# Moving the low halves of the weights by 96 bytes in SBUF: padding in a float32r decoder layer

## Chip, cores and metric

One core of one Trainium2 chip. The metric is the device time of one execution in microseconds (us), the median of several runs. Lower is better.

## What is computed

One decoder layer over 256 tokens of width 1024, in float32: a SwiGLU feed-forward (FFN) of inner width 2816, then a mixing layer with two branches (block attention and RWKV-7) fed by one projection, then a second SwiGLU, then a last RMS norm. Cut to what matters here:

```python
x = x + 0.5 * swiglu(rms_norm(x, norm_ffn1), ffn1_gate, ffn1_up, ffn1_down)
h = rms_norm(x, norm_mix)
proj = h @ w_in                      # 1024 x 5120
...
merged = sigmoid(ga) * (y_a @ proj_a) + sigmoid(gb) * (y_b @ proj_b)
x = x + merged @ w_out               # 1024 x 1024
x = x + 0.5 * swiglu(rms_norm(x, norm_ffn2), ffn2_gate, ffn2_up, ffn2_down)
out = rms_norm(x, norm_final)
```

## The kernel before

**Split products.** Activations lie transposed in SBUF, 128 features of a block on the partitions and 256 tokens along them. Every large product is made in `float32r` from split operands: a weight is `whi + wlo`, an input `hi + lo`, and three TensorE products give the sum. The helper `three` (lines 1445 to 1449) issues them:

```python
mm(dst, whi[slot][:, k_, cols], xl, start=start, stop=False)
mm(dst, wlo[slot][:, k_, cols], xh, start=False, stop=False)
return mm(dst, whi[slot][:, k_, cols], xh, start=False, stop=stop)
```

The first operand is the stationary one (128x128, loaded into the array by a weight load of its own, PEld in the profile), the second the moving one (128x256). The weight load of a product runs while the product before it streams. So the load of a `wlo` block (line 1448) runs beside the product of line 1447, whose moving operand is the low part of the input; both loads of a `whi` block run beside a product whose moving operand is the high part. Lines 1480 to 1482 and 1504 to 1506 issue the same three products through other helpers (they show as L1443), and lines 1594 to 1596 do so for the LoRA weights, which have tensors of their own. The projection chunks 10 and 11 (lines 1714 to 1716) make their result token-major: there the input block is stationary and the weight block moving.

**How many.** The program issues 4632 such products: 2112 for the gates and ups of the two FFNs, 1056 for their downs, 960 for `w_in`, 192 for `proj_a` and `proj_b`, 192 for `w_out`, 120 for LoRA. A third of them, 1544, use a low part of a weight. 1472 of these load `wlo` as the stationary operand, 40 load `lora_wlo`, and 32 have `wlo` as the moving operand.

**The feed of weights.** Weights come in chunks of up to 128x2048 elements, two slots deep. SyncE issues the load to `w_raw` (line 334), ScalarE writes `w_hi` (line 528), VectorE writes `w_lo` as `w_raw - w_hi` (line 896), TensorE multiplies. Each step waits for the one before it, and slots are freed by the `multiplied` and `lo_ready` counts.

**Where things lie.** Tensors are laid in SBUF in the order of their declaration, each rounded up to a multiple of 32 bytes per partition. What a scope frees is used again by the next scope. Every block of 128x256 elements takes 1024 bytes of a partition and every half of it 512, so a tensor's start modulo 256 is also that of all the operands in it.

| tensors | line | start | modulo 256 |
|---|---|---|---|
| `w_raw0`, `w_raw1` | 157 | 16512, 24704 | 128 |
| `w_hi0`, `w_hi1` | 158 | 32896, 41088 | 128 |
| `w_lo0`, `w_lo1` | 159 | 49280, 57472 | 128 |
| `x`, `cst` | 160, 161 | 65664, 73856 | 128 |
| `vec`; `sq`, `sqsum`, `rstd`; `bias_sb`, `idle` | 162 to 168 | from 81824 | 160; 32; 64 |
| `hhi_f`, `hlo_f` (FFN inputs) | 195, 196 | 97440, 105632 | 160 |
| `hid_hi_t`, `hid_lo_t` (inputs of the downs) | 199, 200 | 117920, 140448 | 160 |
| `hhi_m`, `hlo_m` (inputs of `w_in` and LoRA) | 229, 230 | 167072, 175264 | 160 |
| `lora_whi`, `lora_wlo` | 248, 249 | 183680, 204160 | 128 |
| `yahi`, `yalo`, `ybhi`, `yblo`, `mhi`, `mlo` | 227 to 296 | from 158880 | 160 |

So the inputs of all long products begin 32 bytes, modulo 256, behind both halves of the weights.

Of the kernel before, what the change touches and what calls it, by code (L numbers as in the profile page):

```python
# [30 lines left out]
P = 128  # L31
# [113 lines left out]
def trunk(nc, A, consts, out):  # L145
    bias_dram = nc.dram_tensor("bias_rows", (H, 16, 384), F32, kind="Internal").ap()
    with ExitStack() as ctx:
        def sb(name, shape, dt=F32, scope=ctx):
            return scope.enter_context(nc.sbuf_tensor(name, shape, dt))
# [6 lines left out]

        raw = [sb(f"w_raw{i}", [P, KD, W]) for i in range(2)]
        whi = [sb(f"w_hi{i}", [P, KD, W], F32R) for i in range(2)]
        wlo = [sb(f"w_lo{i}", [P, KD, W], F32R) for i in range(2)]
        x = sb("x", [P, KD, T])  # L160
        cst = sb("cst", [P, C_ALL])
# [3 lines left out]

        rstd = sb("rstd", [P, T + 2])
        bias_sb = sb("bias_sb", [H, 384])
        idle = sb("idle", [P, 34])

        def mat(name):  # L170
            return cst[:, CCOL[name]:CCOL[name] + P]
# [1910 lines left out]
```

## Time and profile before

| what | value |
|---|---|
| median of the runs | 635.6 us (635.54, 635.6, 636.8) |
| the profiled execution | 637.97 us, with a span of 636.1 us |
| mean granted TensorE clock in it | 0.998 |

The span runs from the first to the last instruction of the profiled execution; its own time is 1.9 us more, and 2.4 us above the median. In the rows, PE is a TensorE product, PEld a weight load, DVE VectorE, ACT ScalarE, POOL GpSimd, and L1447 is line 1447 of the kernel. The ends of products are modelled by the profiler (a product of 128x256 is shown as lasting 0.28 us, though the next starts long before that), so the pace of the products is read from their starts.

### The profile page before, as it was taken

The numbers are of one execution on the slowest core, as the hardware profiler recorded it, in microseconds if no ns is written. First come the engines' busy times: TensorE is split into PE (matmuls) and PEld (weight loads), VectorE is DVE, ScalarE is ACT, GpSimd is POOL, SyncE is SP. The second block draws the span as 40 slices with busy tenths as digits, with TensorE's granted clock in tenths as the row PEclk, the third lists the DMA queues.
The fourth block names the chain that finished last, engine by engine and source line by source line (L and its number), as shares of the span: only waits on it lengthen the run. The fifth ranks groups of instructions, "written<-read, shape, count | busy, mean of one in ns | idle before, by whom it ended". The sixth has DMA issues, their size and how long they took to land.

```text
span 636.1 us, 15459 instructions
## 1 busy us (share of the span) xinstructions
PE 625.7 (98%) x6720; PEld 611.0 (96%) x6720; DVE 421.7 (66%) x490; ACT 296.0 (47%) x343; POOL 91.3 (14%) x92
## 2 busy tenths in 40 slices
PE   9999999999999999999999999999999999999996
PEld 8899999999999999999988899999999999999996
DVE  5856887665556369968993337878766676665662
ACT  6643555443334264535556445645543344443341
POOL 0017700000114000020015423015000000000120
PEclk9999999999999999999999999999999999999999
DMA  8777566546555246684242233455655566545541
GB/s 280 235 232 209 189 198 197 182 156 203 166 185 186 85 133 199 197 180 154 69 134 70 72 100 100 133 162 172 197 178 176 178 194 198 190 161 201 170 139 66
DMA packets 100672, 105.40 MB, mean 166 GB/s; under 512 B 2244, under 2 KB 98732, under 8 KB 100628
## 3 DMA queue, kind: packets, MB, share of 16 engines
q1 hardware_dynamic: 99380, 101.47, 49.8%
q0 software_dynamic: 1088, 3.02, 2.2%
q8 instruction: 35, 0.57, 0.4%
q10 hardware_dynamic: 160, 0.27, 0.1%
q14 instruction: 9, 0.07, 0.0%
HBM read 103.50 MB, written 1.25 MB: 165 GB/s over the span
## 4 chain that ended last, share of the span: by engine, by line
PE 91%; DVE 4%; DMA 3%; ACT 1%; issue 0%; SPq 0%; DVEq 0%; ACTq 0%
PE two L1447 26%; PE two L1448 25%; PE two L1449 25%; PE two L1443 11%; DMA w_raw<-in_ffn_up 2%; DVE w_lo L896 2%; DMA x_tok<-in_x 1%; PE two L1714 1%; ACT w_hi L528 1%; PE two L1715 1%; PE two L1716 1%; DVE hlo_f L915 1%; PE two L1859 0%; DVE w_lo L906 0%; ACT KK L784 0%
## 5 line engine op out<-in xcount | busy, mean ns | idle before, releaser
L528 ACT ACTIVATE w_hi<-w_raw 128x2048 fp32r<-128x2048 f32 (+1 forms) x87 | 164.3, 1888 | 256.3 <-PE two L1449 232.0
L896 DVE TENSOR_TENSOR w_lo<-w_raw,w_hi 128x2048 fp32r<-128x2048 f32 (+1 forms) x87 | 202.5, 2328 | 86.5 <-ACT w_hi L528 86.1
L1447 PE MATMUL two<-hlo_f,w_hi 128*128 128x256 f32 x640 | 178.9, 280 | 1.6 <-DVE w_lo L896 1.6
L1449 PE MATMUL two<-hhi_f,w_hi 128*128 128x256 f32 x640 | 179.7, 281 | 0.0
L1448 PE MATMUL two<-hhi_f,w_lo 128*128 128x256 f32 x640 | 179.1, 280 | 0.0
L1447 PEld LDWEIGHTS two<-hlo_f,w_hi 128*128 128x128 f32 x640 | 120.5, 188 | 2.7 <-DVE w_lo L896 2.7
L1449 PEld LDWEIGHTS two<-hhi_f,w_hi 128*128 128x128 f32 x640 | 120.4, 188 | 0.0
L1448 PEld LDWEIGHTS two<-hhi_f,w_lo 128*128 128x128 f32 x640 | 120.3, 188 | 0.0
L1447 PE MATMUL two<-hid_lo_t,w_hi 128*128 128x256 f32 x352 | 98.9, 281 | 0.0
L1449 PE MATMUL two<-hid_hi_t,w_hi 128*128 128x256 f32 x352 | 98.6, 280 | 0.0
L1448 PE MATMUL two<-hid_hi_t,w_lo 128*128 128x256 f32 x352 | 98.4, 280 | 0.0
L1447 PE MATMUL two<-hlo_m,w_hi 128*128 128x256 f32 x288 | 83.7, 291 | 0.3 <-DVE w_lo L896 0.3
L1448 PE MATMUL two<-hhi_m,w_lo 128*128 128x256 f32 x288 | 80.6, 280 | 0.8 <-issue 0.8
L1449 PE MATMUL two<-hhi_m,w_hi 128*128 128x256 f32 x288 | 80.5, 279 | 0.0
L1447 PEld LDWEIGHTS two<-hid_lo_t,w_hi 128*128 128x128 f32 x352 | 66.2, 188 | 0.6 <-DVE w_lo L896 0.5
L1448 PEld LDWEIGHTS two<-hid_hi_t,w_lo 128*128 128x128 f32 x352 | 66.2, 188 | 0.0
L1449 PEld LDWEIGHTS two<-hid_hi_t,w_hi 128*128 128x128 f32 x352 | 66.2, 188 | 0.0
L1447 PEld LDWEIGHTS two<-hlo_m,w_hi 128*128 128x128 f32 x288 | 54.2, 188 | 3.0 <-issue 1.4
L1448 PEld LDWEIGHTS two<-hhi_m,w_lo 128*128 128x128 f32 x288 | 54.2, 188 | 1.0 <-issue 1.0
L1449 PEld LDWEIGHTS two<-hhi_m,w_hi 128*128 128x128 f32 x288 | 54.2, 188 | 0.0
L420 POOL TENSOR_TENSOR sqsum<-x 128x512 f32<-128x512 f32 x3 | 3.1, 1041 | 242.9 <-DVE x L1022 214.7
L967 DVE TENSOR_TENSOR prod<-two,rstd 128x512 f32<-128x512 f32 x22 | 15.2, 691 | 24.8 <-PE two L1449 24.8
(336 smaller groups left out, 980.7 us busy)
## 6 DMA issues: line engine op xcount, KB each, us to landing
w_raw<-in_ffn_up SPq DMA_DIRECT2D x21, 1024.0 KB, 5.4
w_raw<-in_ffn_gate SPq DMA_DIRECT2D x20, 1024.0 KB, 5.3
w_raw<-in_w_in SPq DMA_DIRECT2D x20, 1024.0 KB, 5.0
w_raw<-in_ffn_down SPq DMA_DIRECT2D x16, 896.0 KB, 4.6
w_raw<-in_ffn_down SPq DMA_DIRECT2D x8, 1024.0 KB, 5.0
w_raw<-in_w_out SPq DMA_DIRECT2D x4, 1024.0 KB, 5.0
w_raw<-in_proj_a SPq DMA_DIRECT2D x4, 512.0 KB, 3.9
w_raw<-in_proj_b SPq DMA_DIRECT2D x4, 512.0 KB, 4.4
```

Source lines behind the costliest of these rows:

```text
L420: nc.gpsimd.tensor_tensor(sqsum[:], pair, pair, ALU.mult).then_inc(sg["sq_sum"], 1)
L528: nc.scalar.activation(whi[slot][:, 0:kts], raw[slot][:, 0:kts], ACT.Copy).then_inc(sg["hi_ready"], 1)
L896: nc.vector.tensor_tensor(wlo[slot][:, 0:kts], raw[slot][:, 0:kts], whi[slot][:, 0:kts].bitcast(F32), ALU.subtract).then_inc(sg["lo_ready" ...
L915: last = nc.vector.scalar_tensor_tensor(out=hl[:, 2 * j + m], in0=src, scalar=v(GAINS[q], 2 * j + m), in1=hh[:, 2 * j + m].bitcast(F32), o ...
L967: nc.vector.tensor_tensor(prod[:], bank[1][:].rearrange("p (m t) -> p m t", m=2), rstd2, ALU.mult).then_inc(sg["up_taken"], 1)
L1443: return mm(dst, lhsT, rhs, start=start, stop=True, skip_group_check=True)
L1447: mm(dst, whi[slot][:, k_, cols], xl, start=start, stop=False)
L1448: mm(dst, wlo[slot][:, k_, cols], xh, start=False, stop=False)
L1449: return mm(dst, whi[slot][:, k_, cols], xh, start=False, stop=stop)
L1714: mm(dst, hlo_m[:, k_, ts], whi[c % 2][:, k_], start=k_ == 0, stop=False)
L1715: mm(dst, hhi_m[:, k_, ts], wlo[c % 2][:, k_], start=False, stop=False)
L1716: last = mm(dst, hhi_m[:, k_, ts], whi[c % 2][:, k_], start=False, stop=k_ == KD - 1)
```

## The change

One unused tensor of 24 floats (96 bytes per partition) is put between `w_hi` and `w_lo`, and the filler `idle` grows from 34 to 74 floats (160 to 320 bytes with rounding).

```diff
         whi = [sb(f"w_hi{i}", [P, KD, W], F32R) for i in range(2)]
+        sb("pad_w", [P, 24])
         wlo = [sb(f"w_lo{i}", [P, KD, W], F32R) for i in range(2)]
...
-        idle = sb("idle", [P, 34])
+        idle = sb("idle", [P, 74])
```

`w_lo`, `x`, `cst`, `vec`, `sq`, `sqsum`, `rstd`, `bias_sb` and `idle` move up by 96 bytes, everything after `idle` by 256 bytes, which is nothing modulo 256. `w_raw` and `w_hi` stay. `w_lo` then begins at 224 modulo 256, and the inputs of the long products begin 192 bytes behind it, as against 32. No instruction, wait or transfer is added, removed or moved, but one memset (line 1034) writes 74 instead of 34 floats per partition.

## Rows read from the trace of the kernel before

**Rows 1.** The page: busy time by engine, and the granted clock in 40 slices
```profile
PE 625.7 (98%) x6720; PEld 611.0 (96%) x6720; DVE 421.7 (66%) x490; ACT 296.0 (47%) x343; POOL 91.3 (14%) x92
PEclk9999999999999999999999999999999999999999
```

**Rows 2.** The page, chain that ended last; then waits, PE: in total, times, longest
```profile
PE 91%; DVE 4%; DMA 3%; ACT 1%; issue 0%; SPq 0%; DVEq 0%; ACTq 0%
...
PE two L1447 <- DVE w_lo L896: 1.9, 3, 1.0
```

**Rows 3.** Groups by line and shape, PE, products with a low weight part
```profile
L1448 PE MATMUL two<-hhi_f,w_lo 128*128 128x256 f32 x640 | 179.1, 280 | 0.0
...
L1448 PE MATMUL two<-hid_hi_t,w_lo 128*128 128x256 f32 x352 | 98.4, 280 | 0.0
...
L1448 PE MATMUL two<-hhi_m,w_lo 128*128 128x256 f32 x288 | 80.6, 280 | 0.8 <-issue 0.8
...
L1443 PE MATMUL two<-hhi_f,w_lo 128*128 128x256 f32 x64 | 17.9, 280 | 0.0
...
L1715 PE MATMUL two<-w_lo,hhi_m 128*128 128x256 f32 x32 | 9.0, 281 | 0.0
```

**Rows 4.** Timeline (start us, length us), PE and PEld, in FFN 1
```profile
46.15 0.28 PE L1449 MATMUL two<-hhi_f,w_hi 128*128 128x256 f32 x1
...
46.15 0.19 PEld L1447 LDWEIGHTS two<-hlo_f,w_hi 128*128 128x128 f32 x1
46.27 0.19 PEld L1448 LDWEIGHTS two<-hhi_f,w_lo 128*128 128x128 f32 x1
```

**Rows 5.** Timeline, PE: first and last of 768 and of 960 intervals, FFN 1 and 2
```profile
66.05 0.28 PE L1447 MATMUL two<-hlo_f,w_hi 128*128 128x256 f32 x1
...
156.51 0.28 PE L1447 MATMUL two<-hid_lo_t,w_hi 128*128 128x256 f32 x1
...
466.35 0.28 PE L1447 MATMUL two<-hlo_f,w_hi 128*128 128x256 f32 x1
...
579.41 0.28 PE L1447 MATMUL two<-hid_lo_t,w_hi 128*128 128x256 f32 x1
```

**Rows 6.** Timeline, PE: first and last of 288, of 144 and of 96 intervals
```profile
226.20 0.28 PE L1447 MATMUL two<-hlo_m,w_hi 128*128 128x256 f32 x1
...
259.80 0.28 PE L1447 MATMUL two<-hlo_m,w_hi 128*128 128x256 f32 x1
...
402.33 0.28 PE L1447 MATMUL two<-yblo,w_hi 128*128 128x256 f32 x1
...
419.12 0.28 PE L1443 MATMUL two<-mlo,w_hi 128*128 128x256 f32 x1
...
602.22 0.28 PE L1447 MATMUL two<-hid_lo_t,w_hi 128*128 128x256 f32 x1
...
613.42 0.28 PE L1447 MATMUL two<-hid_lo_t,w_hi 128*128 128x256 f32 x1
```

**Rows 7.** Stretches: length, PE busy (count, those in flight at the edges included), clock, DMA
```profile
66.05:156.51 90.46, 90.46 (x771) 1.00 0.57 180
...
226.20:259.80 33.60, 33.60 (x290) 1.00 0.55 181
```

**Rows 8.** Timeline, PE, at a pause in the downs of FFN 2
```profile
600.85 0.28 PE L1449 MATMUL two<-hid_hi_t,w_hi 128*128 128x256 f32 x1
601.06 0.39 PE L1447 MATMUL two<-hid_lo_t,w_hi 128*128 128x256 f32 x1
601.28 0.28 PE L1448 MATMUL two<-hid_hi_t,w_lo 128*128 128x256 f32 x1
```

**Rows 9.** Timeline, PE: first and last of 46 intervals, token-major chunk 10
```profile
277.29 0.28 PE L1715 MATMUL two<-w_lo,hhi_m 128*128 128x256 f32 x1
...
282.73 0.28 PE L1716 MATMUL two<-w_hi,hhi_m 128*128 128x256 f32 x1
```

**Rows 10.** Timeline, PE: the last transposes, and what follows them
```profile
627.43 1.47 PE L2037 MATMUL two<-cst,h_f 128*128 128x128 f32 x12
628.74 0.50 PE L1443 MATMUL two<-cst,sqsum 128*128 128x1 f32 x4
```

## The prediction

> **What bounds the kernel.** I read the page first. TensorE is busy for 98% of the span, its clock is granted in full in all 40 slices, so it runs at the upper of its two levels, 2.4 GHz [rows 1]. The chain that ended last runs 91% through TensorE, and the largest wait that TensorE has in the whole run is 1.9 us, in three pieces [rows 2]. VectorE (66%) and ScalarE (47%) have room. So the time is the sum of the intervals between TensorE's products, and a change that touches no instruction can act only through the length of these intervals, or not at all.
>
> The long products are what fills it. The groups by line and shape give 640 + 64 for the FFNs' gates and ups, 352 for the downs, 288 for most of `w_in` and 32 token-major ones, each standing for one of three passes [rows 3]; with the smaller groups it makes the 4632 of the program. Their shown length of 280 ns is a modelled one and tells nothing, so I went to the timeline and took first and last starts of long unbroken series of the same shape, 128x128 against 128x256. The reader is to see that the same product has three paces:
>
> - FFN 1: 156.51 - 66.05 = 90.46 us over 768 intervals, 117.8 ns each; FFN 2: 113.06 us over 960, 117.8 ns [rows 5]. Unrounded, both are 117.78.
> - `w_in`: 33.60 us over 288, 116.7 ns; the proj and out products: 16.79 us over 144, 116.6 ns; a piece of the downs of FFN 2: 11.20 us over 96, 116.7 ns [rows 6].
> - token-major chunk: 5.44 us over 46, 118.3 ns [rows 9].
>
> At 2.4 GHz 256 columns are 106.7 ns. The paces are 280.0, 282.7 and about 284 clocks, so 24 to 28 clocks of each product are something else. It isn't the clock, and it isn't the other engines: the stretches at 117.8 and at 116.7 have the same clock and the same DMA load, 180 and 181 GB/s [rows 7]. It changes at pauses: the downs of FFN 2 run at 117.8 before a pause at 601.06 and at 116.7 after it, on the same tensors [rows 8, 6]. So a stream of products settles in one of at least two rhythms, and a short pause can throw it from one into the other. What the streams have in common is two readers of SBUF at the same time: each weight load starts with the product before its own, 46.15 with 46.15 [rows 4]. Where they read is what the padding changes.
>
> **The change part by part.**
>
> *The pad before `w_lo`.* It moves the stationary operand of line 1448, so it alters the load that runs beside line 1447, one interval in three: 1472 of the 4632, as the LoRA weights lie elsewhere and the token-major products have `wlo` as the moving operand. The distance from that load to the moving operand goes from 32 to 192 modulo 256. All the other pairs stay at 32.
>
> No row shows a load at 192. The bounds: the transposes also load 128x128 for each product, and 12 of them take 628.74 - 627.43 = 1.31 us, 109.2 ns each [rows 10]. They move 128 columns of plain float32, so they are far, but they show that a load and a product can go by in 109 ns. If every interval with a `wlo` load fell there from about 117.4 (the mean over both rhythms), the gain would be 1472 x 8.2 ns = 12.1 us: the lower end, 623.5. With the same excess once more on top, as for a meeting of the readers twice as costly, it would be 12.1 us lost: 647.7. Between them lie the three paces in the rows, and these are nearest, as they are the same shape, type and pair of readers. They differ by only 1.7 ns. I take their size and keep the outer ends as tails.
>
> *Which pace.* The token-major products are the only ones in the trace with another distance: moving `w_hi` (128), stationary input (160), so -32, or 224, and they are slower by 1.66 ns than the fast rhythm and by 0.55 than the slow one. The distance matters then, or the order of operands does. On the other side, the slow rhythm of the FFNs appears at the same distance 32 as the fast one, and in the timeline it closes over three products, 353.3 ns or 848 clocks, while the fast one is 280 clocks for each. In the slow rhythm three loads with identical distances add 8 clocks per triple. With the change the three are no longer alike; a third of them sits 160 bytes away. I expect that the slow rhythm can't hold itself then and the FFNs run as `w_in` does. This is a choice and not a measurement, and its weak point is that 192 is nearer to the slow 224 than to 32.
>
> *The sum.* About 3070 products run in the slow rhythm: all 3168 of the FFNs but some 270 (about 80 at the very start, some 60 at the head of FFN 2, 130 in the downs), and 168 of LoRA and the first `w_in` chunk. 3070 x 1.11 ns = 3.4 us. The fast ones stay. 637.97 for the profiled execution gives 634.6; the same step from the median, which is 2.4 us below it, gives 635.6 - 3.4 = **632.2**.
>
> *The other tensors that move by 96.* `cst`, `sqsum` and `x` are read by TensorE as plain float32 only: some 16 + 24 + 16 transposes and a few hundred small products. In the transposes a load and a product already take 109.2 ns [rows 10]. Between no change and 8 ns more on some 100 of them this is 0 to 0.8 us; I take 0, since the plain products show no such excess. Reads and writes by VectorE, ScalarE and DMA keep their shapes; I cost them at nothing, because TensorE waits for them 1.9 us in the largest case [rows 2]. A faster TensorE uses the slots sooner, by 48 x 1.11 = 53 ns per chunk of 5.6 us, and the feed has slack: ScalarE and VectorE have a third of the span free or more [rows 1]. The longer memset writes 40 floats more at the start, on VectorE, before the inputs are in: nothing.
>
> **The rivals.**
>
> *No effect.* The rhythm comes from phase at the pauses and not from addresses, and the moved load behaves as any other. For it: both rhythms occur at the same distance [rows 5, 6], the pauses change them [rows 8]. Against it: the token-major pace [rows 9]. Time: 635.6, within the 1.3 us that runs differ. The Trainium skill speaks for it: "TensorE: Matmul & The Clock Gate", Part 2, says of the step LDWEIGHTS that PE has two independent SBUF read ports, and that loading the next weights takes no read bandwidth from the running matmul; by it padding is worth nothing and the time is 635.6. The same page gives the gap of warm products as N/2.4 + 2.5 ns, 109.2 ns for 256 columns, and the trace doesn't agree: no long series here runs under 116.6 ns.
>
> *Slower: the 192 load pays as the one at 224 does.* Place: the load of `wlo` beside line 1447, in all stages. If only that interval in three takes the token-major pace, it is 1472 x about 0.95 ns (118.33 less the mean of 117.4) = 1.4 us: 637.0. If it pulls the whole stream to that pace, 3070 x 0.55 + 1466 x 1.66 ns = 4.1 us: 639.7. If each `wlo` load meets the moving reads once more, at 8 clocks (3.33 ns, the step between 840 and 848 clocks per triple), 1472 x 3.33 = 4.9 us: 640.5. It decides once the mean `wlo` interval rises by more than 2.3 ns, which is the 3.4 us that the FFNs could gain spread over 1472 loads. For it: 192 lies next to 224. I take 639 for it.
>
> *Much faster: the `wlo` load no longer meets the moving reads.* 1472 x 8.2 ns gives 623.5; half of it 629.6. Only the transposes speak for it.
>
> **How the numbers follow.** A measurement of this kernel can tell about 0.2%, 1.3 us, from no change. Forecast (FFNs in the fast rhythm, or a part of them) 0.40 at 632.2; much faster 0.07; no effect 0.20 at 635.6; slower 0.33 at 639. Faster is 0.40 + 0.07 = 0.47, slower 0.33, same 0.20. Cases of both signs hold much of it, so the forecast's own range is 630.5 to 634. The range for 8 in 10 leaves out the much faster case below 628 and the outer half of the costs above 641.5: 628 to 641.5.
>
> **What the profile after would show.** Right: the FFN series at 116.7 ns like `w_in`, the same counts, no new waits, PE still at full clock. Half right: the FFNs gain in one stage only, or `w_in` loses what they gain. Wrong: the interval from line 1447 to line 1448 above 120 ns in all stages (slower), the same 117.8 in FFNs and 116.7 in `w_in` (no effect), intervals under 115 (much faster). A new wait of TensorE for `w_lo` would mean that the feed was nearer to its end than I say.

## The result and the profile after

The changed kernel takes **644.28 us** (median of 4 runs, 643.2 to 644.51) against 635.57 us before: a ratio of 1.0127, 95% interval 1.0109 to 1.0145. It is slower, by 8.7 us. The forecast was 632.2 us with a range of 628 to 641.5.

The page of the kernel after, busy time by engine, the granted clock and the shares of the chain (lines are one higher than before, L1448 is L1447 of before):

```profile
PE 632.8 (98%) x6720; PEld 618.4 (96%) x6720; DVE 421.6 (66%) x490; ACT 296.1 (46%) x343; POOL 92.1 (14%) x92
...
PEclk9999999999999999999999999999999999999998
...
PE 92%; DVE 3%; DMA 3%; ACT 1%; issue 0%; SPq 0%; DVEq 0%; ACTq 0%
```

Beside [rows 1, 2] nothing has changed but PE: 7.1 us more busy time in the same 6720 products, VectorE and ScalarE as before, the clock granted in full. TensorE's waits did not grow either; this is the view of waits, of the kernel after:

```profile
PE two L1444 <- DVE silu L1034: 1.1, 1, 1.1
PE two L1448 <- DVE w_lo L897: 1.0, 2, 0.6
```

So the time sits in the intervals between products. The timeline of the kernel after, first and last start of the same series as in [rows 5, 6]: 768 intervals in FFN 1, 960 in FFN 2, 288 in `w_in`, and then 72 of LoRA with the first projection chunk:

```profile
66.22 0.28 PE L1448 MATMUL two<-hlo_f,w_hi 128*128 128x256 f32 x1
...
157.81 0.28 PE L1448 MATMUL two<-hid_lo_t,w_hi 128*128 128x256 f32 x1
...
466.06 0.28 PE L1448 MATMUL two<-hlo_f,w_hi 128*128 128x256 f32 x1
...
580.55 0.28 PE L1448 MATMUL two<-hid_lo_t,w_hi 128*128 128x256 f32 x1
...
228.05 0.28 PE L1448 MATMUL two<-hlo_m,w_hi 128*128 128x256 f32 x1
...
262.40 0.28 PE L1448 MATMUL two<-hlo_m,w_hi 128*128 128x256 f32 x1
...
207.65 0.28 PE L1444 MATMUL two<-hlo_m,lora_whi 128*128 128x256 f32 x1
...
216.13 0.28 PE L1448 MATMUL two<-hlo_m,w_hi 128*128 128x256 f32 x1
```

| stretch | intervals | before | after |
|---|---|---|---|
| FFN 1 | 768 | 90.46 us, 117.8 ns | 91.59 us, 119.3 ns |
| FFN 2 | 960 | 113.06 us, 117.8 ns | 114.49 us, 119.3 ns |
| `w_in` | 288 | 33.60 us, 116.7 ns | 34.35 us, 119.3 ns |
| LoRA, whose weights did not move | 72 | 8.48 us, 117.8 ns | 8.48 us, 117.8 ns |

The long series whose `w_lo` moved now run at one pace, 119.26 ns unrounded, whatever they had before; the one of LoRA, whose weights did not move, takes the same time to 10 ns. Two short series don't fit this and matter later. The first projection chunk, 48 products right behind LoRA, kept its 117.8 ns although its `w_lo` moved; and the 49 LoRA products right behind the downs of FFN 1 went from 117.8 to 120.0 ns although their weights did not move. The timeline of the kernel after, 45 intervals of that chunk and 45 of those LoRA products:

```profile
215.78 0.28 PE L1448 MATMUL two<-hlo_m,w_hi 128*128 128x256 f32 x1
...
221.08 0.28 PE L1448 MATMUL two<-hlo_m,w_hi 128*128 128x256 f32 x1
...
200.90 0.28 PE L1444 MATMUL two<-hhi_m,lora_whi 128*128 128x256 f32 x1
...
206.30 0.28 PE L1444 MATMUL two<-hhi_m,lora_whi 128*128 128x256 f32 x1
```

The same 45 LoRA intervals in the timeline of the kernel before, 5.30 us as against 5.40:

```profile
198.87 0.28 PE L1443 MATMUL two<-hhi_m,lora_whi 128*128 128x256 f32 x1
...
204.17 0.28 PE L1443 MATMUL two<-hhi_m,lora_whi 128*128 128x256 f32 x1
```

So even 32 throughout can run at 120.0 ns for a while, and 32/192 at 117.8. Added up over all long products, the intervals under 135 ns (4546 before, 4547 after) make 534.1 us before and 541.5 us after, 7.4 us. All the rest got 1.1 us shorter. The spans differ by 6.3 us and not by 8.7, because the profiled execution of before was one of its longer ones (637.97 us against the median of 635.6); why is seen below.

Within a triple, the mean intervals after are (lines of the kernel after) 120.8 ns from line 1448 to 1449 (beside which `w_lo` is loaded), 118.9 to line 1450 and 118.1 back, the same in `w_in` and both FFNs. Before they were 116.4, 116.7 and 117.0 in `w_in`, and 115.8, 118.3 and 119.2 in the FFNs, but with the short one at another place of the triple in FFN 1 than in FFN 2. So the interval with the moved load is the longest now and always in the same place, +4.4 ns in `w_in`, and the two others, beside which the operands that are loaded and streamed lie as before, grow too, by 2.2 and 1.1.

### The profile page after: what moved, and what is told of

It reads as the page before. It is cut to its first block, busy times and chain, and to the rows that moved or that the text cites. A ratio compares the mean times of both kernels' runs of the same rounds, so it can differ in the third digit from the quotient of the medians.

```text
span 642.5 us, 15459 instructions
## 1 busy us (share of the span) xinstructions
PE 632.8 (98%) x6720; PEld 618.4 (96%) x6720; DVE 421.6 (66%) x490; ACT 296.1 (46%) x343; POOL 92.1 (14%) x92
## 4 chain that ended last, share of the span: by engine, by line
PE 92%; DVE 3%; DMA 3%; ACT 1%; issue 0%; SPq 0%; DVEq 0%; ACTq 0%
PE two L1448 27%; PE two L1449 26%; PE two L1450 25%; PE two L1444 11%; DMA w_raw<-in_ffn_up 2%; DVE w_lo L897 1%; DMA x_tok<-in_x 1%; PE two L1715 1%; ACT w_hi L529 1%; PE two L1717 1%; DVE hlo_f L916 1%; PE two L1716 1%; PE two L1860 0%; DVE w_lo L907 0%; ACT KK L785 0%
## 5 line engine op out<-in xcount | busy, mean ns | idle before, releaser
L1448 PE MATMUL two<-hlo_f,w_hi 128*128 128x256 f32 x640 | 181.7, 284 | 1.0 <-DVE w_lo L897 1.0
L1448 PEld LDWEIGHTS two<-hlo_f,w_hi 128*128 128x128 f32 x640 | 120.7, 189 | 2.4 <-DVE w_lo L897 2.4
L1448 PE MATMUL two<-hid_lo_t,w_hi 128*128 128x256 f32 x352 | 100.1, 284 | 0.0
L1448 PE MATMUL two<-hlo_m,w_hi 128*128 128x256 f32 x288 | 84.5, 293 | 0.0
L1448 PEld LDWEIGHTS two<-hid_lo_t,w_hi 128*128 128x128 f32 x352 | 66.3, 188 | 0.4
L1448 PEld LDWEIGHTS two<-hlo_m,w_hi 128*128 128x128 f32 x288 | 54.2, 188 | 2.6 <-issue 1.1
```

## The experiments

All of them but `kick192`, which adds one small product, keep every instruction; only the padding differs. In the diffs `pad_h`, `pad_w` and `pad_x` stand ahead of `w_hi`, `w_lo` and `x`. In all of them the pads ahead of `idle` and what `idle` grows by add up to 256 bytes, so that everything behind `idle` stays where it was modulo 256; beyond that, `e4_follow` pads the inputs too, and `all192` and `kick192` the LoRA weights. "Distance" is the start of the moving operand less that of the stationary one, modulo 256. A name like 32/192 gives that of `w_hi` and of `w_lo`. Each pace is read from the one profiled execution of a kernel; the kernel before ran beside each group of experiments, with medians from 635.2 to 635.9 us.

### Which tensors, and is it the distance of one load

`e1_others`: the pad behind `w_lo`.

```diff
         wlo = [sb(f"w_lo{i}", [P, KD, W], F32R) for i in range(2)]
+        sb("pad_x", [P, 24])
         x = sb("x", [P, KD, T])
...
-        idle = sb("idle", [P, 34])
+        idle = sb("idle", [P, 74])
```

> The pad stands behind w_lo and not ahead of it: x, cst, sq, sqsum and the other small tensors move by 96 bytes as in the change, w_lo stays 32 bytes from the inputs. If the cost comes from the distance between the load of w_lo and the moving operand (theory 1), or from w_lo being unlike w_hi (theory 2): the time of the kernel before, 635.6 us within 1.3, and long products at 116.7 or 117.8 ns as before. If it comes from the other tensors that move (theory 3): 643 to 645 us, products at 119.2 ns or longer pieces elsewhere.

Measured: 635.71 us, ratio 1.0001 (0.9985 to 1.0017). The other tensors cost nothing, theory 3 falls. The profile holds more. The timeline of this kernel, the same 768 and 960 intervals:

```profile
66.16 0.28 PE L1448 MATMUL two<-hlo_f,w_hi 128*128 128x256 f32 x1
...
155.76 0.28 PE L1448 MATMUL two<-hid_lo_t,w_hi 128*128 128x256 f32 x1
...
466.02 0.28 PE L1448 MATMUL two<-hlo_f,w_hi 128*128 128x256 f32 x1
...
578.02 0.28 PE L1448 MATMUL two<-hid_lo_t,w_hi 128*128 128x256 f32 x1
```

89.60 us over 768 and 112.00 over 960: both FFNs run at 116.67 ns here, where the profiled execution of before had 117.78 [rows 5], with the same distances of weights and inputs. Its own time was 634.89 us against 637.97. So neither rhythm belongs to a stage, and 3070 x 1.11 ns = 3.4 us is about the spread of the runs of the kernel before (19 beside this one: 634.39 to 638.08). That its quicker runs have the fast rhythm in the FFNs is inferred from this; only one of its executions was profiled.

`e2_both192` and `e3_hi192`: both halves at 192, and the high half alone.

```diff
+        sb("pad_h", [P, 24])
         whi = [sb(f"w_hi{i}", [P, KD, W], F32R) for i in range(2)]
...
-        idle = sb("idle", [P, 34])
+        idle = sb("idle", [P, 74])
```

```diff
+        sb("pad_h", [P, 24])
         whi = [sb(f"w_hi{i}", [P, KD, W], F32R) for i in range(2)]
+        sb("pad_w", [P, 40])
         wlo = [sb(f"w_lo{i}", [P, KD, W], F32R) for i in range(2)]
```

> w_hi and w_lo both begin 192 bytes from the inputs, so all three loads of a triple are alike again. Theory 1 (each load pays for its own distance to the operand that moves beside it): three intervals of three pay what one paid, 3 x 8.7 us above 635.6, some 655 to 662 us, and about 121 to 124 ns for each product. Theory 2 (a triple pays for having unlike loads, and one distance is as good as another): back to 635 to 638 us, 116.7 to 117.8 ns.

> Only w_hi begins 192 bytes from the inputs, w_lo is at 32 as before, and so are all other tensors. Theory 1: two intervals of three pay, about 2 x 8.7 us, some 651 to 655 us. Theory 2: unlike again in the same proportion, 643 to 646 us.

Measured: 192/192 **630.44 us**, ratio 0.9916 (0.989 to 0.9942), faster than before; 192/32 638.02 us, ratio 1.0036 (1.0024 to 1.0048). Theory 1 asked for 655 to 662 and 651 to 655. It falls: three loads at 192 cost less than none. Theory 2 has the order right and misses both sizes. The timeline of 192/192, FFN 1 (768 intervals), FFN 2 (960) and `w_in` (288):

```profile
66.12 0.28 PE L1448 MATMUL two<-hlo_f,w_hi 128*128 128x256 f32 x1
...
156.58 0.28 PE L1448 MATMUL two<-hid_lo_t,w_hi 128*128 128x256 f32 x1
...
466.02 0.28 PE L1448 MATMUL two<-hlo_f,w_hi 128*128 128x256 f32 x1
...
574.83 0.28 PE L1448 MATMUL two<-hid_lo_t,w_hi 128*128 128x256 f32 x1
...
228.03 0.28 PE L1448 MATMUL two<-hlo_m,w_hi 128*128 128x256 f32 x1
...
260.67 0.28 PE L1448 MATMUL two<-hlo_m,w_hi 128*128 128x256 f32 x1
```

FFN 2 and `w_in` go at 113.33 ns, 272 clocks of 2.4 GHz, quicker than anything before; FFN 1 goes at 117.8. This pair of distances has two rhythms too, 4.45 ns apart. In the profile of 192/32 both `w_in` and FFN 2 run at 117.78 ns, and pieces of the downs at 117.1.

`e4_follow`: the kernel after, with the low halves of the inputs moved along (the same lines for `hid_lo` and `hlo_m`).

```diff
+            sb("pad_f1", [P, 24], scope=sc)
             hlo_f = sb("hlo_f", [P, KD, T], F32R, scope=sc)
+            sb("pad_f2", [P, 40], scope=sc)
```

> The kernel after, with the low halves of the inputs (hlo_f, hid_lo, hlo_m) moved by the same 96 bytes as w_lo. The load of w_lo then runs again beside an operand 32 bytes away, the loads of w_hi too; but w_lo is 192 bytes from the operand that it is itself multiplied with, and w_hi of line 1447 is 128 from its own. Theory 1 (it is the load against the product that streams beside it): back to 635 to 637.5 us, products at 116.7 or 117.8 ns in the FFNs and w_in; the 384 proj and out products stay at about 119.2. Theory 4 (the load against its own product, or w_lo against w_hi): 643 us or more.

Measured: 641.72 us, ratio 1.0088 (1.0063 to 1.0114). FFN 1 runs at 118.53 ns, `w_in` at 117.78, and the proj and out products, whose inputs were not moved, at 119.2. Neither side got its number. Moving the operand that streams beside the load of `w_lo` does help, by 0.7 to 1.5 ns, but with all three simultaneous pairs 32 bytes apart most of the FFNs still doesn't get back to 117.78. It isn't the simultaneous pair alone. Two other things are still unlike before, and the run doesn't separate them: the distance of an operand to its own product (192 for `w_lo`, 128 for the `w_hi` of the first product), and operands that jump from one residue to another between products.

### One distance throughout

`pad_h` of 8, 56, 48, 40, 32 or 16 floats and `idle` of 98 less that, for 0, 64, 96, 128, 160 and 224.

> w_hi and w_lo both 224 (that is, -32) from the inputs, everything else as before modulo 256. Working theory now: a stream of products has a few stable rhythms, which follow from the whole set of distances, and pauses choose among them. 32/32 has 116.67 and 117.78 ns, 192/192 has 113.34 and 117.78. If the token-major chunk, with -32 and the roles swapped, stood for this distance: one rhythm near 118.3 ns and 638 to 641 us. If each distance had a price that adds up by pairs: 224 next to 192 would be about as cheap as 192/192, 630 us.

> Both halves of the weights begin at the same place modulo 256 as the inputs. If the two readers meet where their addresses agree modulo 256, this one meets at the start of every product and is the slowest of the uniform distances: over 118 ns, over 640 us. If only likeness counts: 634 to 638 us.

> Both halves 64 bytes from the inputs. If likeness is all that counts: 634 to 638 us, 116.7 or 117.8 ns. If the distance counts by itself, as 192/192 showed with 113.34 ns, this can be anything between 113.3 and 119 ns; a neighbour of 32 should be near it, 116 to 118 ns.

> Both halves 128 bytes from the inputs, the farthest that 256 allows. If the readers are cheapest when farthest apart: 113.3 ns or less in all stages, 617 to 630 us. If likeness is all: 634 to 638 us.

> Both halves 160 bytes from the inputs. So far the pace of a stream with one distance throughout goes with that distance: 0 gives 120.0 ns, 32 gives 116.67 or 117.78, 64 gives 117.78, 128 gives 118.65, 192 gives 113.33 or 117.78, 224 gives 118.33, and the token-major chunk follows the same table with its own distance. 160 lies between 128 and 192: if the table is smooth there, 115 to 118 ns, 628 to 640 us; if 192 is a single notch, 118 ns or more and 640 us. The token-major chunk has distance 96 in this kernel and shows its pace beforehand.

> Both halves 96 bytes from the inputs, between 64 (117.78 ns) and 128 (118.65 ns): 117.8 to 118.7 ns and 637 to 643 us if the table is smooth. The token-major chunk of this kernel has distance 160 and must show the pace of the run with both halves at 160, and the other way round.

| distance | 0 | 32 (before) | 64 | 96 | 128 | 160 | 192 | 224 |
|---|---|---|---|---|---|---|---|---|
| pace in the profile, ns | 120.00 | 116.67, 117.78 | 117.78 | 120.00 | 118.67 | 117.33, 118.67 | 113.33, 117.78 | 118.33 |
| median, us | 646.32 | 635.6 | 637.54 | 646.44 | 642.02 | 638.79 | 630.44 | 641.21 |

The medians of 0, 96, 128 and 224 are of two runs each, the others of three to eight. The runs of 64 lie from 633.43 to 638.82, so it may have a faster rhythm that its profile (637.76 us) doesn't show. The paces are those of the long series; at 160 one chunk of 48 products in FFN 1 ran at 120.1 ns.

The distance by itself is worth 16 us from best to worst, and the order is not smooth: 96 costs as much as 0 and 128, the farthest, is no optimum. Neighbours are not alike: 96 against 64, 192 against 224.

What does hold is the crossed pair. In the token-major chunks the weight is the moving operand, so their distance is the negative one, and each kernel of this row measures a second distance in them. The timeline, token-major chunk 10, 45 intervals, in the kernels with both at 64, at 224 and at 96:

```profile
277.01 0.28 PE L1716 MATMUL two<-w_lo,hhi_m 128*128 128x256 f32 x1
...
282.13 0.28 PE L1716 MATMUL two<-w_lo,hhi_m 128*128 128x256 f32 x1
```
```profile
280.10 0.28 PE L1717 MATMUL two<-w_hi,hhi_m 128*128 128x256 f32 x1
...
285.35 0.28 PE L1717 MATMUL two<-w_hi,hhi_m 128*128 128x256 f32 x1
```
```profile
280.93 0.28 PE L1717 MATMUL two<-w_hi,hhi_m 128*128 128x256 f32 x1
...
286.20 0.28 PE L1717 MATMUL two<-w_hi,hhi_m 128*128 128x256 f32 x1
```

Both at 64 makes the chunk -64 = 192: 5.12 us over 45 is 113.8 ns, the fast rhythm of 192. Both at 224 makes it 32: 5.25 us, 116.7 ns. Both at 96 makes it 160: 5.27 us, 117.1 (117.3 unrounded). Both at 160 makes it 96, and it takes 120.0; both at 192 makes it 64, and it takes 117.8. Five of five agree with the table (chunk 11 of the kernel with both at 64 took 117.8, the slow rhythm of 192), and the row of before does too: its chunk at 224 took 118.3 ns [rows 9], and 224 throughout takes 118.33, from the timeline of that kernel, 960 intervals of FFN 2 in 113.60 us:

```profile
466.31 0.28 PE L1448 MATMUL two<-hlo_f,w_hi 128*128 128x256 f32 x1
...
579.91 0.28 PE L1448 MATMUL two<-hid_lo_t,w_hi 128*128 128x256 f32 x1
```

So the pace of a stream with one distance follows the start of the moving operand less that of the loaded one, modulo 256, whatever tensors they are. That the period is 256 and not 512 shows in `e1_others`: its inputs lie 288 bytes behind the weights modulo 512, those of before 32, and `w_in` runs at 116.7 ns in both. Whether it is the product beside a load or the load's own product that counts can't be told here, as the two distances are the same in all these kernels. In clocks of 2.4 GHz, three products take 816, 840, 848, 852 and 864 for 113.33, 116.67, 117.78, 118.33 and 120.00 ns.

### `w_lo` alone

`pad_w` of 56, 48, 40, 32, 16 or 8 floats, for `w_lo` at 64, 96, 128, 160, 224 and 0, and `idle` of 98 less that; the change itself is the one of 24.

> Only w_lo at 64, w_hi stays at 32. Each of the two distances alone gives 116.67 or 117.78 ns. If a triple pays the mean of its three distances (theory 1): 116.7 to 117.8 ns, 633 to 638 us. If unlike distances cost by themselves, as 32/192 showed (119.24 where the mean of the parts is 115.6 to 116.3): 118.5 ns or more, 640 us or more.

> Only w_lo at 224, w_hi stays at 32. The mean of the parts is (2 x 116.67 to 117.78 + 118.33) / 3 = 117.2 to 118.0 ns, 635 to 639 us (theory 1). If unlike distances cost 3 ns more, as in the change: 120 to 121 ns, 648 to 652 us.

> Only w_lo at 0, w_hi at 32. Uniform 0 gives 120.0 ns. Mean of the parts: (2 x 116.67 to 117.78 + 120.0) / 3 = 117.8 to 118.5 ns, 636 to 641 us. If unlike distances cost about 3 ns by themselves: 121 ns, 650 us.

> Only w_lo at 128, as far (96 bytes) from w_hi as in the change, on the other side. Mean of the parts: (2 x 116.67 to 117.78 + 118.67) / 3 = 117.3 to 118.1 ns, 635 to 640 us. If it is the step of 96 bytes between the loads that costs: 119.2 ns, 644 us or more.

> Only w_lo at 160, 128 bytes from w_hi, the farthest. Mean of the parts: (2 x 116.67 to 117.78 + 117.33 to 118.67) / 3 = 116.9 to 118.1 ns, 634 to 640 us. If steps between the loads cost: 119 ns or more, 643 us or more.

> Only w_lo at 96, 64 bytes from w_hi. Mean of the parts: (2 x 116.67 to 117.78 + 120.0) / 3 = 117.8 to 118.5 ns, 636 to 641 us. If steps cost with their size, between those of 32 bytes (nothing: 32/64 and 32/224 stood at 117.77, the mean of their parts) and of 96: 119 to 120 ns, 643 to 648 us.

| `w_lo` at, with `w_hi` at 32 | 0 | 32 (before) | 64 | 96 | 128 | 160 | 192 (the change) | 224 |
|---|---|---|---|---|---|---|---|---|
| pace in FFN 2, ns | 117.04 | 117.78 | 117.78 | 117.78 | 117.78 | 118.89 | 119.26 | 117.78 |
| mean of its parts, ns | 117.8 to 118.5 | 116.67, 117.78 | 117.0 to 117.8 | 117.8 to 118.5 | 117.3 to 118.1 | 116.9 to 118.1 | 115.6 to 117.8 | 117.2 to 118.0 |
| median, us | 638.33 | 635.6 | 640.11 | 638.41 | 638.94 | 642.17 | 644.28 | 638.5 |

Two rows of the timeline of 32/128, which has the same step of 96 bytes between the loads as the change; 960 intervals of FFN 2 in 113.07 us, 117.78 ns:

```profile
466.01 0.28 PE L1448 MATMUL two<-hlo_f,w_hi 128*128 128x256 f32 x1
...
579.08 0.28 PE L1448 MATMUL two<-hid_lo_t,w_hi 128*128 128x256 f32 x1
```

That settles the size of the step: by itself it isn't what costs (here it is one down, in the change one up). Five of the seven mixtures lie at 117.78 or under it in FFN 2, as the mean of the parts allows (0 comes out 0.8 ns under it), and their medians are 2.7 to 4.5 us above before. But the FFN 2 row alone doesn't price a mixture, as mixtures have several rhythms too: 32/0 runs `w_in` at 118.9 ns, above its mean, and 32/64 runs a part of the downs of FFN 2 at 118.8. Otherwise the five hold 117.78 nearly throughout. What all seven, and 192/32, have in common is that none runs the bulk of `w_in` at the 116.67 ns that it has before: it takes 117.8 or more in each. The change, 32/192, is the worst of all, 1.5 ns above the upper end of the mean of its parts, and 32/160 comes next. The same distance that is the best of all when all three loads have it is the worst of this row when the load of `w_lo` alone has it.

### A version that beats both, and whether a pause chooses the rhythm

`all192`: 192/192, and the LoRA weights at 192 as well. `kick192`: the same with one small product behind the fourth chunk.

```diff
-                mb("pad_lora", [P, 24], scope=sc)
+                mb("pad_lora", [P, 48], scope=sc)
```
```diff
                     chunk(1, 1)
+                    part(bank[7][:, 0:2], ident, cst[:, C_EPS:C_EPS + 2], True)
```

> Every half of every weight, the LoRA ones too, 192 bytes from the inputs; the candidate to beat both kernels. With w_hi and w_lo at 192 and LoRA at 32 it was 630.4 us. The 120 LoRA products and the first projection chunk can gain up to 168 x 4.4 ns = 0.7 us more: 629 to 631.5 us. If the rhythm of FFN 1 is drawn anew in each run, the times spread from 622 to 634.

> The same, with one small product (128x128 on 2 columns, into a bank that nothing reads) behind the fourth chunk of FFN 1, 6 us after the pause from which both192 went on at 117.78 ns. If pauses choose the rhythm, the stream of FFN 1 may come out of this one at 113.33 ns: 1120 x 4.45 ns = 5.0 us less, 624.5 to 626 us; or it stays where it is, 629.5 to 631.5 us. If the stage itself holds the slow rhythm (its addresses or its loop), it stays at 117.78 whatever the small product does.

Measured: `all192` **625.31 us**, ratio 0.9833 (0.9815 to 0.985), below the 629 to 631.5 expected, inside the wider spread; five of its six runs lie from 623.88 to 626.32, with a median of 625.07, and one at 634.21. `kick192` 625.79 us, ratio 0.9851 (0.9831 to 0.9871). In the timeline of `all192`, FFN 1 now has the fast rhythm (576 intervals in 65.28 us, 113.33 ns), and so has FFN 2:

```profile
66.00 0.28 PE L1448 MATMUL two<-hlo_f,w_hi 128*128 128x256 f32 x1
...
131.28 0.28 PE L1448 MATMUL two<-hlo_f,w_hi 128*128 128x256 f32 x1
```

It didn't come from the LoRA products: 71 of the 120 run at 117.8 ns in it, and the 49 at 113.4 are worth 0.2 us. In FFN 1 every operand lies where it lay in `e2_both192`, where it ran at 117.8; 1216 x 4.45 ns = 5.4 us comes near the difference of the two medians, 5.1. So the stage doesn't hold the slow rhythm. Whether pauses choose it `kick192` can't tell, as its partner was already in the fast one. The four runs of `e2_both192` lie within 1.2 us, and those of `all192` within 2.4 but for the one at 634, so for these two the rhythm is not drawn freely in each run. They ran on different chips (the kernel before took 635.6 and 635.9 us on them), and a rival that no run rules out is that the chip takes part in the choice. What decides it stays open.

## Why the prediction was wrong

**What bounds the kernel** was right: TensorE's intervals alone, no waits, no clock, no other engine. The counts of products were right as well.

**The step that failed** is "Which pace": "With the change the three are no longer alike; a third of them sits 160 bytes away. I expect that the slow rhythm can't hold itself then and the FFNs run as `w_in` does." The runs show the reverse. Unlike loads don't free a stream from its slow rhythm. In all eight kernels with unlike halves and unmoved inputs `w_in` lost its 116.67 ns; five of them hold the slow 117.78 there instead, and 32/192 runs at 119.26 ns in `w_in` and the FFNs alike. In place of 3070 x -1.11 ns, the products of the slow rhythm without the 120 of LoRA lost 2950 x 1.48 ns = 4.4 us, and the other 3.0 of the 7.4 us fell on some 1400 products that I had costed at nothing, 2.6 ns each in `w_in`.

What the runs say of the other steps, in their order:

- "They differ by only 1.7 ns. I take their size": the trace of before showed three paces and I took them for the scale. One distance throughout spans 113.33 to 120.00 ns, 6.7 ns. The outer bounds (623.5 and 647.7) held, the range between them was cut too narrow.
- The slow rhythm in the FFNs was read as a mark of those stages. `e1_others` has the fast one there, at the same distances, and its profiled execution took 634.89 us: about the 634.6 that *The sum* gets from the profile for FFNs in the fast rhythm. So 634.6 was all that this mechanism could give. The 632.2 took the 3.4 us once more from a median that lay 2.4 us below the profiled execution, and that probably had a part of the gain in it already.
- The slower rival had the place right (the interval beside line 1447, in all stages) and came nearest with its 4.9 us, but reasoned that 192 "lies next to 224". Nearness is no guide here: 192 throughout is the best and 224 is 5 ns slower. It had 0.33 and 639; the loss was 1.8 times its largest price.
- **No effect** fell: addresses alone move the kernel from 625 to 646 us. The other tensors that move by 96 bytes cost nothing, as the prediction had it.

The Trainium skill, "TensorE: Matmul & The Clock Gate", Part 2, says that PE has two independent SBUF read ports and that loading the next weights takes no read bandwidth from the running matmul. These `float32r` streams don't bear it out: the same instructions at the same clock take from 113.33 to 120.00 ns by the distance of the two operands, though no run shows which of the two reads is held up. The gap of N/2.4 + 2.5 ns, 109.2 here, which that page of the Trainium skill calls the one of an isolated product, was reached by none of them.

The token-major row was worth more than I made of it. I used it as an argument that 192 might be slow. It turned out to be the pace of 224 throughout, and the kernel had no such row for 192.

**What stays open.** Why a distance has the pace it has, why one load of three at 192 costs more than the mean of its parts, and what picks between the rhythms of one layout. The two short series beside LoRA suggest that a stream can keep a rhythm from the products before it, but no run tests that. `e4_follow` shows that the operand beside a load counts and that it isn't all; it doesn't tell a load's own product from the jump of residues between products.

## What to carry to other kernels

Where TensorE streams long `float32r` products with a weight load each, read the pace from the starts in the timeline (shown lengths are modelled) and vary the start of the stationary operands against the moving ones in steps of 32 bytes modulo 256: here it is worth 3.4% between the best and the worst, for a line of padding. Move all stationary operands of the stream together first; a distance that is best for all can be worst for one of three, so a pair priced alone may mislead. And a kernel may have two rhythms at one layout: look at several executions before you call a stage slow.

## What was not expected of the hardware

- The pace goes with the distance in a jagged row (120.00, 116.67, 117.78, 120.00, 118.67, 117.33, 113.33, 118.33 ns for 0 to 224, the faster rhythm where there are two) and follows moving less stationary, with the sign: 32 and 224 differ by 1.7 ns, 64 and 192 by 4.4.
- Rhythms last: 1216 products in a row at 117.78 ns in FFN 1 of before, without a change. The changes on unchanged tensors that were seen lie at pauses, as the one at 601.06 us of before [rows 8], and many pauses leave a rhythm as it is.
- LoRA products of the kernel after, at unchanged distances, ran at 120.0 ns behind a stream at 119.26, and at 117.8 a pause later.
- Two kernels whose FFN operands lie at the same addresses, `e2_both192` and `all192`, settle in different rhythms of FFN 1, 5.1 us apart, with runs that agree among themselves but for one.
